# Gathering the experts' tokens by one float32 product instead of two products on split values

## The reference, cut to what matters

```python
logits = (h @ w_r).astype(jnp.float32) + b_r.astype(jnp.float32)
top_v, top_i = lax.top_k(logits, TOP_K)
probs = jax.nn.softmax(top_v, axis=-1)
combine = jnp.einsum('blk,blke->ble', probs, jax.nn.one_hot(top_i, N_EXPERTS, dtype=jnp.float32))
out = jnp.zeros_like(h)
for e in range(N_EXPERTS):
    out = out + combine[..., e, None].astype(h.dtype) * swiglu(h, w1[e], w3[e], w2[e])
```

## Time and profile before

| | |
|---|---|
| median of 3 runs | 1560.74 us |
| the profiled execution, first to last instruction | 1559.4 us |
| TensorE busy (weight loads apart) | 1477.2 us, 95% |
| VectorE, ScalarE busy | 838.9 us, 617.5 us |
| DMA, mean over the span | 254 GB/s |

### The profile page before, as it was taken

One profiled execution on the slowest core, in us unless ns is written; L12 is line 12 of the kernel. 1 busy time (PEld: TensorE's weight loads), 2 busy tenths in 40 slices (PEclk: granted clock), 3 DMA queues, 4 the chain that ended last, 5 costly groups with the idle time before them and its releaser, 6 DMA issues.

```text
span 1559.4 us, 21947 instructions
## 1 busy us (share of the span) xinstructions
PE 1477.2 (95%) x8714; PEld 1041.6 (67%) x8715; DVE 838.9 (54%) x1135; ACT 617.5 (40%) x698; POOL 17.4 (1%) x56
## 2 busy tenths in 40 slices
PE   5999798999999999897879999999999999999997
PEld 3786486788888887783755566565766566565754
DVE  2899945333333333799564554445554555545552
ACT  3425723322122222439344333434443444434442
POOL 2000000000000000100010000000000000000000
PEclk8999899999999999999889999999999999999998
DMA  9633933921542233348159999989999999999992
GB/s 360 199 100 106 363 108 129 236 75 56 146 116 78 69 93 125 102 142 331 49 217 395 340 330 337 343 323 407 381 408 405 403 385 401 408 379 404 383 409 105
DMA packets 208006, 395.44 MB, mean 254 GB/s; under 512 B 12044, under 2 KB 123040, under 8 KB 207904
## 3 DMA queue, kind: packets, MB, share of 16 engines
q1 hardware_dynamic: 207312, 393.80, 70.2%
q10 hardware_dynamic: 592, 0.21, 0.1%
HBM read 392.93 MB, written 1.05 MB: 253 GB/s over the span
## 4 chain that ended last, share of the span: by engine, by line
PE 87%; DVE 4%; ACT 4%; DMA 2%; issue 2%; DVEq 0%; ACTq 0%
PE bank L757 85%; PE bank L1248 1%; DMA raw<-in_w_mod 1%; DMA raw<-in_moe_w 1%; DVE tb L1828 1%; ACT la L1532 1%; DVE y L1957 0%; DVE h_lo L1836 0%; ACT lr L1526 0%; PE bank L1193 0%; DMA rows_sb<-in_b_mod 0%; ACT lm L1574 0%; PE bank L782 0%; ACT li L1528 0%; ACT lm L1539 0%
## 5 line engine op out<-in xcount | busy, mean ns | idle before, releaser
L2265 DVE TENSOR_TENSOR w_lo<-raw,w_hi 128x2048 fp32r<-128x2048 f32 x132 | 302.4, 2292 | 260.5 <-ACT w_hi L1653 260.5
L1653 ACT ACTIVATE w_hi<-raw 128x2048 fp32r<-128x2048 f32 x132 | 252.4, 1912 | 402.1 <-PE bank L757 285.5
L757 PE MATMUL bank<-h_hi,w_hi 128*128 128x512 f32 (+1 forms) x768 | 285.2, 371 | 13.1 <-DVE h_lo L1836 12.0
L757 PE MATMUL bank<-h_lo,w_hi 128*128 128x512 f32 (+1 forms) x768 | 283.0, 368 | 0.0
L757 PE MATMUL bank<-h_hi,w_lo 128*128 128x512 f32 (+1 forms) x768 | 282.9, 368 | 0.0
L1411 ACT ACTIVATE w_hi<-raw 128x2048 fp32r<-128x2048 f32 (+1 forms) x64 | 113.7, 1776 | 209.8 <-PE bank L757 196.0
L757 PEld LDWEIGHTS bank<-h_hi,w_hi 128*128 128x128 f32 x768 | 147.2, 192 | 38.8 <-DVE h_lo L1836 13.4
L757 PEld LDWEIGHTS bank<-h_lo,w_hi 128*128 128x128 f32 x768 | 147.2, 192 | 23.5
L757 PEld LDWEIGHTS bank<-h_hi,w_lo 128*128 128x128 f32 x768 | 146.9, 191 | 23.5
L1811 DVE TENSOR_TENSOR w_lo<-raw,w_hi 128x2048 fp32r<-128x2048 f32 (+1 forms) x64 | 136.0, 2124 | 36.8 <-ACT w_hi L1411 36.6
L757 PE MATMUL bank<-w_hi,hc_hi 128*128 128x512 f32 (+1 forms) x384 | 153.1, 399 | 2.4 <-ACT warm L1708 2.4
(11 more groups left out here) (307 smaller groups left out, 1796.6 us busy)
## 6 DMA issues: line engine op xcount, KB each, us to landing
raw<-in_moe_w SPq DMA_DIRECT2D x220, 1024.0 KB, 9.0
raw<-in_w_mod SPq DMA_DIRECT2D x48, 1024.0 KB, 8.7
raw_x<-in_moe_w SPq DMA_DIRECT2D x44, 1024.0 KB, 8.9
raw<-in_ffn_w SPq DMA_DIRECT2D x44, 512.0 KB, 5.3
raw<-in_w_in SPq DMA_DIRECT2D x18, 1024.0 KB, 5.4
raw<-in_ffn_w SPq DMA_DIRECT2D x16, 704.0 KB, 4.5
raw<-in_w_out SPq DMA_DIRECT2D x8, 1024.0 KB, 5.7
x_in<-in_ctx SPq DMA_DIRECT2D x1, 1024.0 KB, 5.0
```

The source lines that it names most:

```text
L757: return nc.tensor.matmul(dst, lhsT, rhs, start=first, stop=last)
L1653: nc.scalar.activation(w_hi[:, j % SPL, :], raw[:, E_SLOT[j], :], ACT.Copy)\
L2265: V.tensor_tensor(w_lo[:, j % SPL, :], raw[:, E_SLOT[j], :], w_hi[:, j % SPL, :].bitcast(F32), ALU.subtract).then_inc(dve_done, dve_n(name ...
```

## The change

The rows of the tokens are kept once, in float32 (`ht`), without a low part; `picks` is float32 too. A block of 128 features is gathered by two float32 products instead of four `fp32r` ones. The split into high and low part is made behind the gather: ScalarE rounds what was gathered to `hc_hi`, and VectorE subtracts `hc_hi` from the gathered PSUM block to give `hc_lo`. There are four groups a turn instead of eight, three at chunk 23 and one at chunk 26, none at chunk 29. The waits for the last `next_hc` become waits for VectorE's last `next_hc_lo`. In the first gather, ScalarE makes its four copies and then the three roundings of weights; VectorE no longer makes `ht_lo` and no longer adds.

```diff
@@ -87,8 +87,10 @@
 TURN_AT = {0: 9, 1: 11, 2: 17, 3: 19, 4: 23, 5: 25}
 SEL_AT, PICK_AT = 5, 14
 
-GATHER_AT = {23: (0, 1, 2), 26: (3, 4, 5), 29: (6, 7)}
+GATHERS = KD // 2
+GATHER_AT = {23: (0, 1, 2), 26: (3,)}
 GATHER_BANK = (0, 1, 5)
+FIRST_BANK = 2
 
 XCAP = 32
...
@@ -282,8 +284,7 @@
 
         cursor[0] = area
         hT = sb("hT", [P, KD, NX])
-        ht_hi = sb("ht_hi", [P, 2, D], F32R)
-        ht_lo = sb("ht_lo", [P, 2, D], F32R)
+        ht = sb("ht", [P, 2, D])
         selT = sb("selT", [P, NX], F32R)
         hc_hi = sb("hc_hi", [P, KD, CAP], F32R)
...
@@ -342,7 +343,7 @@
         all1 = sb("all1", [P, P])
         iota_s = sb("iota_s", [P, CAP])
         iota_x = sb("iota_x", [P, P])
-        picks = sb("picks", [P, 2, 3 * P], F32R)
+        picks = sb("picks", [P, 2, 3 * P])
         hcx = sb("hcx", [P, KD, XCAP])
         lgT = nc.alloc_sbuf_tensor_at("lgT", [P, NX], F32, offset=cursor[0])
...
@@ -1093,23 +1094,22 @@
 
             def gather(n, s):
 
-                part, w = n // 4, gather_width(s)
+                w = gather_width(s)
                 for kk in range(2):
-                    k = 2 * (n % 4) + kk
+                    k = 2 * n + kk
                     for t in range(2):
-                        i = mm(bank[GATHER_BANK[n % 3]][:, w * kk:w * kk + w], (ht_hi, ht_lo)[part][:, t, P * k:P * k + P],
+                        i = mm(bank[GATHER_BANK[n % 3]][:, w * kk:w * kk + w], ht[:, t, P * k:P * k + P],
                                picks[:, t, P:P + w], t == 0, t == 1)
                 i.then_inc(pe_done, pe_n("next_gather", n))
 
-            def first_gather(part, b):
-
-                src = (ht_hi, ht_lo)[part]
+            def first_gather():
+
                 for k in range(KD):
                     for t in range(2):
-                        i = mm(bank[b + k // 2][:, JW * (k % 2):JW * (k % 2) + JW], src[:, t, P * k:P * k + P],
+                        i = mm(bank[FIRST_BANK + k // 2][:, JW * (k % 2):JW * (k % 2) + JW], ht[:, t, P * k:P * k + P],
                                picks[:, t, JOINT], t == 0, t == 1)
                     if k % 2:
-                        i.then_inc(pe_done, pe_n("first_gather", part, k // 2))
+                        i.then_inc(pe_done, pe_n("first_gather", k // 2))
 
             def back(blocks, done, count, name, x=False, s=False):
...
@@ -1294,7 +1294,7 @@
                     i.then_inc(pe_done, pe_n("e_mm", j))
 
                 if not first:
-                    pe.wait_ge(act_done, at("next_hc", 7) - Ka + ae)
+                    pe.wait_ge(dve_done, at("next_hc_lo", GATHERS - 1) - Kd + de)
                     if s:
                         pe.wait_ge(s_dve, at("s_hc") - Ksd + sd)
                 for j in range(PER_EXPERT):
@@ -1338,27 +1338,25 @@
                                 pe.wait_ge(s_dve, at("s_sel") + sd)
                                 pe.wait_ge(s_dve, at("s_hid", 2) + sd)
                         if n >= 3:
-                            pe.wait_ge(act_done, at("next_hc", n - 3) + ae)
+                            pe.wait_ge(dve_done, at("next_hc_lo", n - 3) + de)
                             if s:
                                 pe.wait_ge(s_dve, at("s_part", n - 3) + sd)
                         gather(n, s)
                 if not s:
                     pe.wait_ge(dve_done, at("e_y", 1) + de)
-                    pe.wait_ge(act_done, at("next_hc", 7) + ae)
+                    pe.wait_ge(dve_done, at("next_hc_lo", GATHERS - 1) + de)
 
             pe.wait_ge(dve_done, at("first_sel"))
             pe.wait_ge(x_dve, at("x_sel"))
...
-            first_gather(0, 4)
-            pe.wait_ge(dve_done, at("ht_lo"))
-            first_gather(1, 0)
+            pe.wait_ge(act_done, at("ht_sb", 1, 1))
+            first_gather()
 
             Ksd, Ksa = at("per_s", "dve"), at("per_s", "act")
             pe.wait_ge(x_dve, at("x_hc"))
             for j in range(AHEAD):
                 x_mm(j)
-            pe.wait_ge(act_done, at("first_hc", 1, 3))
+            pe.wait_ge(dve_done, at("first_hc_lo", GATHERS - 1))
             pe.wait_ge(s_dve, at("s_first_hc"))
             n0, ns0 = pe_n.n, spe_n.n
...
@@ -1640,8 +1638,8 @@
             for t in range(2):
                 for half in range(2):
                     act.wait_ge(pe_done, at("ht", t, half))
-                    nc.scalar.activation(ht_hi[:, t, 512 * half:512 * half + 512], bank[2 * t + half][:, :], ACT.Copy)\
-                        .then_inc(act_done, act_n("ht_hi", t, half))
+                    nc.scalar.activation(ht[:, t, 512 * half:512 * half + 512], bank[2 * t + half][:, :], ACT.Copy)\
+                        .then_inc(act_done, act_n("ht_sb", t, half))
 
             Kp, Kd, Ka = (at("per_expert", x) for x in ("pe", "dve", "act"))
...
@@ -1746,25 +1744,17 @@
                         x_step(j)
                     for n in GATHER_AT.get(j - 1, ()):
                         act.wait_ge(pe_done, at("next_gather", n) + pp)
-                        k = 2 * (n % 4)
-                        nc.scalar.activation((hc_hi, hc_lo)[n // 4][:, k:k + 2, :], gathered(n, s)[:, :, 0:CAP], ACT.Copy)\
+                        nc.scalar.activation(hc_hi[:, 2 * n:2 * n + 2, :], gathered(n, s)[:, :, 0:CAP], ACT.Copy)\
                             .then_inc(act_done, act_n("next_hc", n))
                     if s:
                         s_step(j, turn_no)
 
-            def first_gathered(part, b):
-                for n in range(4):
-                    act.wait_ge(pe_done, at("first_gather", part, n))
-                    if part:
-                        act.wait_ge(s_dve, at("s_first_hc", n) if n < 3 else at("s_first_hc"))
-                    nc.scalar.activation((hc_hi, hc_lo)[part][:, 2 * n:2 * n + 2, :],
-                                         bank[b + n][:, 0:2 * JW].rearrange("p (k c) -> p k c", k=2)[:, :, XCAP:XCAP + CAP],
-                                         ACT.Copy).then_inc(act_done, act_n("first_hc", part, n))
-
-            first_gathered(0, 4)
-            e_hi(0, 0, 0, "first_hi")
-            first_gathered(1, 0)
-            for j in range(1, SPL):
+            for n in range(GATHERS):
+                act.wait_ge(pe_done, at("first_gather", n))
+                nc.scalar.activation(hc_hi[:, 2 * n:2 * n + 2, :],
+                                     bank[FIRST_BANK + n][:, 0:2 * JW].rearrange("p (k c) -> p k c", k=2)[:, :, XCAP:XCAP + CAP],
+                                     ACT.Copy).then_inc(act_done, act_n("first_hc", n))
+            for j in range(SPL):
                 e_hi(j, 0, 0, "first_hi")
             n0, ns0 = act_n.n, sact_n.n
...
@@ -2408,16 +2398,14 @@
                     else:
                         V.memset(nil[:, n - PER_EXPERT:n - PER_EXPERT + 1], 0.0)\
                             .then_inc(dve_done, dve_n("next_lo", n - PER_EXPERT))
-                    for n in GATHER_AT.get(j - 1, ()) if s else ():
+                    for n in GATHER_AT.get(j - 1, ()):
+                        two = slice(2 * n, 2 * n + 2)
                         dve.wait_ge(act_done, at("next_hc", n) + ae)
-                        dst = hcs[:, 2 * (n % 4):2 * (n % 4) + 2, :]
-                        src = gathered(n, s)[:, :, CAP:CAP + SCAP]
-                        if n < 4:
-                            i = V.tensor_copy(dst, src)
-                        else:
-                            dve.wait_ge(s_dve, at("s_part", n - 4) + turn_no * at("per_s", "dve"))
-                            i = V.tensor_tensor(dst, src, dst, ALU.add)
-                        i.then_inc(s_dve, sdve_n(*(("s_part", n) if n < 7 else ("s_hc",))))
+                        V.tensor_tensor(hc_lo[:, two, :], gathered(n, s)[:, :, 0:CAP], hc_hi[:, two, :].bitcast(F32),
+                                        ALU.subtract).then_inc(dve_done, dve_n("next_hc_lo", n))
+                        if s:
+                            V.tensor_copy(hcs[:, two, :], gathered(n, s)[:, :, CAP:CAP + SCAP])\
+                                .then_inc(s_dve, sdve_n(*(("s_part", n) if n < GATHERS - 1 else ("s_hc",))))
                     if top and j in MORE_AT:
                         (full_experts, more_turns, more_columns)[MORE_AT.index(j)]()
...
@@ -2469,33 +2457,15 @@
             V.tensor_copy(cw1[:, :, :], comb[:, :, column]).then_inc(dve_done, dve_n("first_cw"))
             V.tensor_copy(cw1_s[:, :, :], comb[:, :, column_s]).then_inc(s_dve, sdve_n("s_first_cw"))
 
-            for t in range(2):
-                for half in range(2):
-                    cols = slice(512 * half, 512 * half + 512)
-                    dve.wait_ge(act_done, at("ht_hi", t, half))
-                    V.tensor_tensor(ht_lo[:, t, cols], bank[2 * t + half][:, :], ht_hi[:, t, cols].bitcast(F32),
-                                    ALU.subtract).then_inc(dve_done, dve_n(*(("ht_lo",) if t and half else ())))
-
-            def first_gathered(part, b):
-                for n in range(4):
```

(27 more changed lines are left out.)

7 lines of the change are left out of this document (3 added, 4 removed).

## The result

The changed kernel takes 1571.49 us (median of 4 runs, 1569.02 to 1572.0) against 1560.99 us for the kernel before beside it: a ratio of 1.0057 [1.0043, 1.0071]. Run again on another occasion it gave 1569.84 us, 1.0051 [1.0037, 1.0064]. The ratios are estimated from all runs of an occasion and are not quotients of the two medians. By the ratios the change costs 8.9 and 8.0 us; the medians themselves lie 10.5 and 7.6 us apart (the second beside 1562.26 us). Forecast were +9.2 us and 1569.9 us, with 1566 to 1575 us as the range.

A forecast was written before the change was run, and what follows sets the result against it. TensorE was taken to bound the turns, a chain over TensorE, ScalarE and VectorE the opening. Turns 6.4 us plus first gather 2.8 us gave +9.2 us on 1560.7 us: 1569.9 us, range 1566 to 1575 us.

The forecast's parts named there:

- A record of 192 columns, 0.162 us: Gathers in the turns: each float32 record of 192 columns costs 0.162 us, 0.045 us longer than the present ones.
- The lower bound: Gather records in the turns: weight loading alone, 0.117 us a record.
- the upper: Gather records in the turns: 0.216 us a record, if width counted for nothing.
- The sum of a turn, +1.6: Gathers at chunks 23, 26 and 29: +2.49, -0.01 and -0.89, +1.6 us a turn, +6.4 us in four.
- The opening, +3.4 less 0.6: First gather to first split product: +3.4 us by ScalarE's later w_hi, 0.6 us recovered from later waits, +2.8 us.
- The cover at chunk 25, costed at nothing: Transpositions at chunk 25 wait for hd_lo behind three more subtractions; an earlier rounding restores the cover, 0 us.
- The chance of 0.08 for this rival: Rival at chunk 25: VectorE's subtractions hold the transpositions, +2.5 us, 1572.4 us; chance 0.08.
- The clock stays low through the gather: Rival in the opening: TensorE at half clock through the whole first gather, +3.9 us, 1573.8 us; chance 0.12.
- Records at the cost of a load: Rival on narrow float32 records: 192 columns cost 0.117 us, the turns cost nothing, 1560.9 us; chance 0.05.
- Loads not hidden: Rival on gather records: float32 loads add about 0.11 us to each of 32, +13.7 us, 1583.6 us; chance 0.03.
- A gain by waits not seen: Rival, place not given: more time hides a landing TensorE indirectly waits for, 1556 us; chance 0.02.

The follow-up runs named there:

- the opening alone: Kernel before with only the first gather in float32 and the new order of ScalarE's and VectorE's work ahead of turn 0: 1564.19 us, 1.0014.
- the order repaired: Changed kernel with ScalarE's rounding of chunk 0 moved back behind its second copy: 1567.81 us, 1.0038.
- the clock repaired: Changed kernel with eight extra float32 products, results unread, on TensorE ahead of the first gather: 1567.44 us, 1.0042.
- both together: Changed kernel with the early rounding of chunk 0 and the eight extra products ahead of the first gather: 1567.24 us, 1.0034.

## Why the prediction was right

- **A record of 192 columns, 0.162 us.** Measured 0.1625 us. The rule behind it, width by 0.84 ns, held at 160 and 256 columns too. The lower bound was a little high (0.112 us is the floor, at 64 and at 128 columns), the upper is what 256 columns take. This one number carries 6.5 us of the loss.
- **The sum of a turn, +1.6.** By groups: chunk 23 was forecast at +2.49 and came to +2.45, with +0.12 at chunk 24; chunk 26 at -0.01, and is -0.15 with +0.11 at chunk 27; chunk 29 at -0.89, and is -0.98 with +0.11 at chunk 30. The 0.11 behind each is only where the cut between the chunks falls, since the first record of a chunk is listed 0.11 us behind the start of an old gather record and only 0.03 us behind that of a float32 one, which makes the chunk behind an old gather shorter. Turn 1: +1.61.
- **The opening, +3.4 less 0.6.** It was +3.18 (3.30 in the profile with the opening alone) less 0.56. The chain was the one described: gather 8.3 us at two clocks, four copies, `w_hi`, `w_lo`, product. The 0.1 to 0.2 too much lies in the end of the gather (the last copy ended at 8.7 us behind the gather's start and not at 8.8) and in copies that overlap the rounding's start; it is within the spread of the openings from profile to profile. The experiments add what the forecast could not know: the order of ScalarE is worth 1.1 us alone, the low clock 2.0 us. With the order repaired the three x products end last, with the clock repaired `w_lo` does.
- **The cover at chunk 25, costed at nothing.** Right in its result, with a delay of at most 0.02 us in any turn, but by luck. The waits of ScalarE for weights did shrink; between 1022 and 1200 us they are

```profile
ACT w_hi L1651 <- DMA raw<-in_moe_w: 18.4, 6, 4.0
```

  (us in total, times, longest), where the kernel before had 38.8 us in 14 times. The rounding in question no longer waits for a landing. But it then waits 5.24 us for TensorE to release its slot, and is only 0.5 us earlier against the chunk (3.22 us behind the start of chunk 24, 3.72 before). Three subtractions at 0.33 us are 1.0 us. Of these the earlier rounding took up 0.5 and the later start of chunk 25 (0.12 us behind chunk 24's) 0.12; the other 0.38 came out of the 0.44 us of cover, of which the hand-over needs 0.06: all of it. I had not asked what releases the rounding once the landing doesn't. The chance of 0.08 for this rival was too small for a cover that came out at nothing.
- **Half clock at the start of turn 3, not foreseen.** 1.56 us in the profile of the changed kernel. The forecast took TensorE's clock as full all through the turns, although the edge of the loop, with 2.4 us of idle, was there to be read. In the profile it offsets the early start of the gather in part: 6.5 (four gathers) + 3.18 - 0.56 + 1.56 - 2.64 = 8.0, and the span grew by 7.9. So the profile's number comes near the forecast's because these two, which the forecast did not have, take each other back in part. In the timed runs neither is known for each execution. Without both it is 6.5 + 2.6 = 9.1 us, 0.58%, next to 0.57% and 0.51% measured; with the half-clock stretch in every execution it would be 0.68%, within the first interval and outside the second.
- **The rivals.** *The clock stays low through the gather*: it rose after 4 us, as before. *Records at the cost of a load*: refuted at 192 columns, and right under some 133. *Loads not hidden*: refuted by the sum of the records; 24 records in 3.77 us leave no 0.11 us beside each. The prediction tied this rival to present pairs that load several times faster; that step does not hold, as said with the widths, and the pairs start 0.112 us apart like the float32 records at the floor. *A gain by waits not seen*: the DMA waits that went were not on TensorE's path.

## What to carry to other kernels

A split into high and low part is worth its second product per tile only where the product is wide enough: four `fp32r` products of 192 columns took 4 x 0.112 us where two float32 products take 4 x 0.1625, though both count four records. At 128 columns and below the float32 record, at 0.112 us, would have cost no more than those. At 256 columns the gap is wider still: at full clock the `fp32r` records on `y_hi` and `y_lo` start 0.120 us apart, those of float32 0.216. Price a product by the distance of starts at its width, not by the mean length of its record. And when an opening is a chain over three engines, undo its parts one by one and together: here each repair alone returned 1 or 2 us, both together 3.2, and part of that was taken again by the next wait.

## What the hardware showed that was not expected

- Records of a float32 product on a 128 by 128 tile start 0.112 us apart at 64 and 128 columns, 0.136 at 160, 0.1625 at 192 and 0.216 at 256: a floor up to some 133 columns (an estimate from these), then 0.84 ns a column, at 2.4 GHz. `fp32r` records of 192 columns start 0.112 us apart and those of 256 columns 0.120.
- The edge between two passes of a loop of the turns' size costs TensorE about 2.4 us (the chunk ahead of it took 7.1 to 7.5 us instead of 4.85 in 11 profiles), and in 4 of the 11 it was followed by 3 us at half clock, 1.6 us more. Two turns of straight code in its place took 0.9965 [0.9952, 0.9979] on the kernel before.
- Products put ahead of a loop to fill its idle didn't overlap it: 3.96 us of them were followed by 5.36 us of idle, where it had been 3.79.
- Where TensorE waited for `hd_lo`, its transpositions started 0.055 us after the end of VectorE's instruction. A distance of that size in a trace is no cover.
- Subtractions from PSUM of 128x256 that are listed with 0.42 us start 0.33 us apart.
